# Conditioning weights dealt over three feed-forward stages instead of two, with VectorE's share of that work in smaller portions

## The reference, cut to what matters

```python
for l in range(DEPTH):
    mod_lat = (silu(c) @ w_ada[l] + b_ada[l]).reshape(b, 9, D)
    mod_ctx = (silu(c_ctx) @ w_ada[l] + b_ada[l]).reshape(1, 9, D)
    x  = _post(x,  _swiglu(_pre(x,  g[0], mod_lat, 0), ffn1_gu[l], ffn1_down[l]), g[1], mod_lat, 0, 0.5)
    xc = _post(xc, _swiglu(_pre(xc, g[0], mod_ctx, 0), ffn1_gu[l], ffn1_down[l]), g[1], mod_ctx, 0, 0.5)
    ...
    x  = _post(x,  _swiglu(_pre(x,  g[4], mod_lat, 2), ffn2_gu[l], ffn2_down[l]), g[5], mod_lat, 2, 0.5)
```

## Time and profile before

| what | value |
| --- | --- |
| median of 3 runs | 2853.93 us (2853.24 to 2855.41) |
| the profiled execution, its own time | 2855.19 us |
| its span | 2853.2 us, granted clock 0.969 |
| TensorE matmul busy | 2685.9 us, 94% of the span |
| VectorE busy | 1676.4 us, 59% |
| ScalarE, GpSimd busy | 716.0 us, 25%; 819.5 us, 29% |
| shares of the chain that ended last | TensorE 84%, VectorE 11%, of it adaW L541 3% |

### The profile page before, as it was taken

How to read it: one execution, slowest core, us unless ns; L and a number is a source line. 1 busy time by engine, 2 the same in 40 slices (tenths; PEclk the granted TensorE clock), 3 DMA queues, 4 the chain that set the end, 5 groups by cost and what they waited for, 6 DMA issues and landing times.

```text
span 2853.2 us, 39518 instructions
## 1 busy us (share of the span) xinstructions
PE 2685.9 (94%) x16446; PEld 2502.7 (88%) x16446; DVE 1676.4 (59%) x2235; ACT 716.0 (25%) x977; POOL 819.5 (29%) x1292
## 2 busy tenths in 40 slices
PE   5999999998899889999999799999999799899997
PEld 4899999998779789999999699999999668588885
DVE  5867876875582676766765643343344694644444
ACT  4211121112423431111111322112212324322222
POOL 1247776641050200000000227757641041100001
PEclk9899999999999999999999899999999899899998
DMA  9443444442445134344342232223223456133331
GB/s 315 126 132 123 152 137 142 126 165 97 138 154 163 52 104 126 107 129 126 104 126 82 74 74 80 91 91 97 82 93 111 158 160 192 59 96 96 96 96 52
DMA packets 340457, 337.07 MB, mean 118 GB/s; under 512 B 52528, under 2 KB 311224, under 8 KB 336696
## 3 DMA queue, kind: packets, MB, share of 16 engines
q1 hardware_dynamic: 279224, 204.07, 24.4%
q10 hardware_dynamic: 51840, 77.07, 8.1%
q0 software_dynamic: 9216, 53.42, 5.0%
HBM read 290.02 MB, written 44.50 MB: 117 GB/s over the span
## 4 chain that ended last, share of the span: by engine, by line
PE 84%; DVE 11%; ACT 2%; issue 2%; DMA 0%; POOL 0%; SPq 0%; ACTq 0%; DVEq 0%; POOLq 0%
PE ps L454 74%; DVE adaW L541 3%; PE ps L1394 2%; PE ps L582 2%; PE ps L1089 2%; ACT wH L439 1%; PE ps L1419 1%; DVE tmpN L1168 1%; DVE wL L446 1%; DVE rmsX L1177 1%; DVE xT L1049 1%; PE ps L1361 1%; PE ps L1074 1%; PE ps L1408 1%; DMA xin<-in_x_dram 0%
## 5 line engine op out<-in xcount | busy, mean ns | idle before, releaser
L454 PE MATMUL ps<-hH,wH 128*128 128x384 f32 (+1 forms) x2928 | 1020.1, 348 | 54.4 <-DVE hL L1186 48.1
L454 PE MATMUL ps<-hL,wH 128*128 128x384 f32 (+1 forms) x2928 | 1012.5, 346 | 0.0
L454 PE MATMUL ps<-hH,wL 128*128 128x384 f32 (+1 forms) x2928 | 1011.9, 346 | 0.0
L446 DVE TENSOR_TENSOR wL<-raw,wH 128x1024 fp32r<-128x1024 f32 x300 | 392.4, 1320 | 542.1 <-ACT wH L439 541.6
L454 PEld LDWEIGHTS ps<-hH,wH 128*128 128x128 f32 x2928 | 556.7, 190 | 81.1 <-issue 55.7
L454 PEld LDWEIGHTS ps<-hL,wH 128*128 128x128 f32 x2928 | 556.6, 190 | 17.9
L454 PEld LDWEIGHTS ps<-hH,wL 128*128 128x128 f32 x2928 | 556.1, 190 | 18.4
L454 PE MATMUL ps<-midH,wH 128*128 128x384 f32 (+1 forms) x1232 | 426.9, 346 | 12.6 <-DVE wL L446 9.9
L454 PE MATMUL ps<-midH,wL 128*128 128x384 f32 (+1 forms) x1232 | 424.2, 344 | 0.0
L454 PE MATMUL ps<-midL,wH 128*128 128x384 f32 (+1 forms) x1232 | 424.2, 344 | 0.0
L439 ACT ACTIVATE wH<-raw 128x1024 fp32r<-128x1024 f32 x300 | 310.7, 1050 | 420.8 <-PE ps L454 399.3
(11 more groups left out here) (257 smaller groups left out, 2384.9 us busy)
## 6 DMA issues: line engine op xcount, KB each, us to landing
raw<-in_ffn_gu_dram SPq DMA_DIRECT2D x176, 512.0 KB, 3.9
adaW<-in_w_ada_dram ACTq DMA_DIRECT2D x40, 1536.0 KB, 6.9
raw<-in_ffn_down_dram SPq DMA_DIRECT2D x88, 512.0 KB, 3.6
x_d<-xT POOLq DMA_DIRECT2D x4, 3072.0 KB, 9.6
xT<-x_d POOLq DMA_DIRECT2D x4, 3072.0 KB, 11.0
W_d<-gW POOLq DMA_DIRECT2D x16, 512.0 KB, 3.9
VT_d<-gVT ACTq DMA_DIRECT2D x16, 512.0 KB, 3.0
raw<-in_w_in_dram SPq DMA_DIRECT2D x16, 512.0 KB, 6.0
```

Source lines behind the costliest of these rows:

```text
L446: nc.vector.tensor_tensor(wL[:, n % SPLIT_SLOTS, :], raw[:, n % RAW_SLOTS, :], wH[:, n % SPLIT_SLOTS, :].bitcast(f32), ALU.subtract).then_ ...
L454: ins = nc.tensor.matmul(dst, a, b, start=first and n == 0, stop=last and n == 3 * len(pairs) - 1)
```

## The change

Rides 8 to 21 are put in FFN A, 22 to 33 in FFN B, 34 to 47 in FFN C. VectorE's steps come in portions behind its own work ("hooks"): up to 4 behind each `split_lo` and each `up` of a round, and one behind each addition L747. A ride's column sums stand on TensorE ahead of the first unit that finds all 16 steps early enough in VectorE's order, and this can be any of the four units; an up unit's columns are taken by ScalarE in `up`.

```diff
+    HOOK_SHARES = (4, 4, 4, 4) + (1,) * KC
+    LEAD_SHARES = (0, 0, 2, 4)
+    def share_after(s, hook):
+        if s < 0:
+            return sum(LEAD_SHARES[:hook + 1])
+        return sum(LEAD_SHARES) + s * sum(HOOK_SHARES) + sum(HOOK_SHARES[:hook + 1])
+    def share_before_unit(s, i):
+        if i == 3:
+            return share_after(s, 0)
+        return share_after(s - 1, (4 + 3, 4 + 6, 4 + KC - 1)[i] if s else i)
+    LAST_SHARE = share_before_unit(NPH - 2, 3)
+    def steps_due(n_rides, share):
+        return min(STEPS * n_rides, STEPS * n_rides * share // LAST_SHARE)
+    def place_rides(rides):
+        units = [(s, i) for s in range(NPH - 1) for i in range(4)]
+        at = {}
+        for k, R in enumerate(rides):
+            at[next(u for u in units if steps_due(len(rides), share_before_unit(*u)) >= STEPS * (k + 1) and u not in at)] = R
+        return at
...
-    F1_0 = make_ffn("f10", 0, ffn1_gu, ffn1_down, 0, 8, True)
+    F1_0 = make_ffn("f10", 0, ffn1_gu, ffn1_down, 0, range(8, 22), True)
-    F2_0 = make_ffn("f20", 0, ffn2_gu, ffn2_down, 0, 28, False)
-    F1_1 = make_ffn("f11", 1, ffn1_gu, ffn1_down, 0, None, True)
+    F2_0 = make_ffn("f20", 0, ffn2_gu, ffn2_down, 0, range(22, 34), False)
+    F1_1 = make_ffn("f11", 1, ffn1_gu, ffn1_down, 0, range(34, 48), True)
...
+        def free_tile(g):
+            if g >= F.slots:
+                wait_tile(pe, F, g - F.slots)
+            if g - F.slots in ride_in:
+                pe.wait_ge(ada_taken, ride_in[g - F.slots] + 1)
...
+        def take_ride(g, ride):
+            if ride is not None:
+                take_columns(act, ride, 2 * tile_slot(F, g), TOK // 2)
+                next_ride(ride + 2)
...
-        def up(i, f):
+        def up(i, g, f, ride):
             act.wait_ge(up_read, F.n0["up_read"] + f + 1)
+            take_ride(g, ride)
             nc.scalar.activation(midH[:, f % 4, F.tok0:TOK], midF[:, f % 2, F.tok0:TOK], ACT.Copy).then_inc(mid_hi, 1)
...
+        def ada_until(s, hook):
+            if not F.rides:
+                return
+            n = len(F.rides)
+            for step in range(steps_due(n, share_after(s, hook - 1)), steps_due(n, share_after(s, hook))):
+                ada_step_of(dve, F.rides[step // STEPS], step % STEPS)
...
             for m in range(KC):
-                if ride is not None:
-                    ada_steps(dve, ride, KC + m, KC + m + 1)
...
                                         sb_pair(yT[:, m, :], F.tok0), ALU.add).then_inc(down_read, 1)
+                if p < NPH - 1:
+                    ada_until(p, 4 + m)
...
         for s in range(NPH - 1):
-            more = F.ride0 is not None and s < NPH - 2
-            if F.ride0 is not None:
-                ada_steps(dve, F.ride0 + 2 * s + 1, 0, STEPS)
             for j in range(2):
-                if j and more:
-                    ada_steps(dve, F.ride0 + 2 * s + 2, 0, KC)
                 split_lo(dve, F.base + i + 3)
+                ada_until(s, 2 * j)
                 up(i + 1, g + 1, f)
-            down(8 + 6 * s, 8 + 12 * s, s, F.ride0 + 2 * s + 2 if more else None)
+                ada_until(s, 2 * j + 1)
+            down(8 + 6 * s, 8 + 12 * s, s)
```

More of the change, by code:

```diff
@@ L232, in build @@
     unit = 0
+    STEPS = 2 * KC
     NPH = FC // 2
@@ L338, in make_spill, with make_ffn @@
         return made["spill"]
-    def make_ffn(tag, layer, gu, down, tok0, ride0, gen):
+    def make_ffn(tag, layer, gu, down, tok0, rides, gen):
         nonlocal unit
         F = Section("ffn", FFN_COUNTS)
-        F.tag, F.layer, F.tok0, F.ride0, F.base = tag, layer, tok0, ride0, unit
+        F.tag, F.layer, F.tok0, F.base = tag, layer, tok0, unit
+        F.rides = rides
+        F.ride_of = place_rides(rides)
         unit += 6 * (FC // 2)
@@ L381, in build @@
     pre_first.sq = sq_first
-    F1_0 = make_ffn("f10", 0, ffn1_gu, ffn1_down, 0, 8, True)
+    F1_0 = make_ffn("f10", 0, ffn1_gu, ffn1_down, 0, range(8, 22), True)
     M0 = make_mixer("m0", 0, F1_0.gen)
-    F2_0 = make_ffn("f20", 0, ffn2_gu, ffn2_down, 0, 28, False)
-    F1_1 = make_ffn("f11", 1, ffn1_gu, ffn1_down, 0, None, True)
+    F2_0 = make_ffn("f20", 0, ffn2_gu, ffn2_down, 0, range(22, 34), False)
+    F1_1 = make_ffn("f11", 1, ffn1_gu, ffn1_down, 0, range(34, 48), True)
     M1 = make_mixer("m1", 1, F1_1.gen)
-    F2_1 = make_ffn("f21", 1, ffn2_gu, ffn2_down, CTX, None, False)
+    F2_1 = make_ffn("f21", 1, ffn2_gu, ffn2_down, CTX, range(0), False)
     plan = []
@@ L510, in build @@
     FIRST_RIDES = 8
-    FFN_RIDES = 20
     def ada_source(layer, ride_in_layer):
@@ L519, in ada_dma, with ada_step_of @@
         act.dma_start(adaW[:, R % 2, :, :], ada_source(*divmod(R, RIDES))).then_inc(ada_ready[R % 2], 16)
-    STEPS = 2 * KC
-    def ada_steps(dve, R, first, last):
+    def ada_step_of(dve, R, i):
         before = STEPS * (R - FIRST_RIDES)
         w = adaW[:, R % 2]
[L528 to L542, removed]
+        k, v = i // 2, 1 - i % 2
+        needed = before + (i if i < 4 else i - 1)
+        if needed:
+            dve.wait_ge(ada_step, needed)
+        if i == 0:
+            dve.wait_ge(ada_ready[R % 2], 16 * ((R - FIRST_RIDES) // 2 + 1))
+            ins = nc.vector.tensor_scalar(adaP[:], w[:, 0], siluC[:, 0, 0:1], None, ALU.mult)
+        elif i == 1:
+            ins = nc.vector.tensor_scalar(w[:, 0], w[:, 0], siluC[:, 0, 1:2], None, ALU.mult)
+        else:
+            at = w[:, 1 - v]
+            ins = nc.vector.scalar_tensor_tensor(at, w[:, k], siluC[:, k, v:v + 1], adaP[:] if i == 3 else at, ALU.mult,
+                                                 ALU.add)
+        ins.then_inc(ada_step, 1)
     def ada_ride(pe, R, bank, col):
@@ L612, in ffn_tensor, with gate_up @@
     def ffn_tensor(pe, F, pre):
-        def gate_up(i, g, ride):
+        ride_in = {4 + 12 * s + i: R for (s, i), R in F.ride_of.items()}
+        def free_tile(g):
             if g >= F.slots:
                 wait_tile(pe, F, g - F.slots)
+            if g - F.slots in ride_in:
+                pe.wait_ge(ada_taken, ride_in[g - F.slots] + 1)
+        def gate_up(i, g, ride):
+            free_tile(g)
             if ride is not None:
@@ L631, in down @@
             for m in range(KC):
-                wait_tile(pe, F, g + m - F.slots)
+                free_tile(g + m)
                 for h, (t0, w) in enumerate(halves(F.tok0)):
@@ L646, in ffn_tensor @@
             for i in range(4):
-                ride = F.ride0 + 2 * s + i // 2 if F.ride0 is not None and i % 2 == 0 else None
-                gate_up(4 + 6 * s + i, 4 + 12 * s + i, ride)
+                gate_up(4 + 6 * s + i, 4 + 12 * s + i, F.ride_of.get((s, i)))
             piece = s - 1 if F.gen and 1 <= s <= PIECES else None
@@ L671, in next_ride @@
         def next_ride(R):
-            if R < F.ride0 + FFN_RIDES:
+            if R in F.rides:
                 ada_dma(act, R)
-        if F.ride0 is not None:
[L677 to L683, removed]
+        def take_ride(g, ride):
             if ride is not None:
@@ L686, in gate @@
                 next_ride(ride + 2)
+        if F.rides:
+            act.wait_ge(h_lo, KC * F.pre.nth + KC)
+            next_ride(F.rides[0])
+            next_ride(F.rides[0] + 1)
+        def gate(i, g, f, ride):
+            act.wait_ge(w_used, F.base + i + 1)
+            take_ride(g, ride)
             if f >= 2:
@@ L700, in ffn_scalar @@
             gate(2 * j, 2 * j, j, None)
-            up(2 * j + 1, j)
+            up(2 * j + 1, 2 * j + 1, j, None)
         for s in range(NPH - 1):
             for j in range(2):
-                i, f = 4 + 6 * s + 2 * j, 2 + 2 * s + j
-                gate(i, 4 + 12 * s + 2 * j, f, None if F.ride0 is None else F.ride0 + 2 * s + j)
-                up(i + 1, f)
+                i, g, f = 4 + 6 * s + 2 * j, 4 + 12 * s + 2 * j, 2 + 2 * s + j
+                gate(i, g, f, F.ride_of.get((s, 2 * j)))
+                up(i + 1, g + 1, f, F.ride_of.get((s, 2 * j + 1)))
             piece = s - 1 if F.gen and 1 <= s <= PIECES else None
@@ L735, in up, with down @@
                                     midH[:, f % 4, F.tok0:TOK].bitcast(f32), ALU.subtract).then_inc(mid_lo, 1)
-        def down(i, g, p, ride=None):
+        def ada_until(s, hook):
[4 more added lines that the diff above has]
+                ada_step_of(dve, F.rides[step // STEPS], step % STEPS)
+        def down(i, g, p):
             for m in range(KC):
-                if ride is not None:
-                    ada_steps(dve, ride, KC + m, KC + m + 1)
                 if m < KC - 1:
@@ L753, in ffn_vector @@
         for j in range(2):
-            if F.ride0 is not None:
-                ada_steps(dve, F.ride0, j * KC, (j + 1) * KC)
             split_lo(dve, F.base + 2 * j + 3)
+            ada_until(-1, 2 * j)
             up(2 * j + 1, 2 * j + 1, j)
+            ada_until(-1, 2 * j + 1)
         for s in range(NPH - 1):
-            more = F.ride0 is not None and s < NPH - 2
```

(8 more changed lines are left out.)

## The result

| | before | after |
| --- | --- | --- |
| median | 2854.11 us (4 runs) | 2872.11 us (4 runs, 2869.49 to 2874.42) |
| ratio | | 1.0064, 95% interval 1.0052 to 1.0076 |
| profiled execution, its span | 2855.19, 2853.2 us | 2871.68, 2869.9 us |
| granted clock | 0.969 | 0.972 |
| DVE busy | 1676.4 us | 1667.8 us |

Forecast was 2866 us, range 2842 to 2886. In the chain of waits of the changed kernel (start us, length us, engine tile line, instructions) the ends of the three FFNs are found as in the earlier trace rows. L485 is the line of the matmuls now, L609 that of the column sums, L792 that of the additions, L769 and L773 those of `midF` and `midL`.

A forecast was written before the change was run, and what follows sets the result against it. TensorE, 94% busy, was taken to lose 30.6 us in FFN A to late VectorE. -29.9 - 0.6 + 33.5 + 3.4 + 5.4 = +11.8 us on 2855.2; by the median 2866 us, range 2842 to 2886.

The forecast's parts named there:

- Taken away: TensorE's waits for VectorE's ride steps and additions, with slowed matmuls behind them, go: -29.9 us in FFN A, -0.6 in B.
- cover of 0.3 us: FFN B: tile 4 due at 1092.7, addition 0 done at 1092.3 with three more steps, so no cost there.
- The fourth portion: Four steps behind a round's last `up` delay down tile 3 in FFN A and C: +33.5 us; ScalarE's column-taking +3.4.
- The margin of 0.26 us: FFN A, down tile 3: slack before the first addition delays TensorE if no step stands ahead; four steps cost 1.86 us.
- GpSimd beside the steps: VectorE steps before the first addition fall in GpSimd's quiet part, 0.53 us each; its large operations could stretch them.
- The other end: Steps before the first addition take 1.09 us each in every round, beside GpSimd's large operations: 40 us more.
- Loads: Rounds 1 and 3 of FFN A and C: VectorE waits some 4 us for ride loads; cost 0, at worst 16 us.
- The clock: TensorE's clock falls behind three of eighteen new waits at down tile 3: +5.4 us, ends 0 and 32.
- the bracket: TensorE idle gaps: 1.5 us left the clock alone, 2.45 us cost 1.8 us; the new waits lie between.
- The not-slower one: TensorE's waits for steps go and steps before the first addition cost nothing: 2823 us; with a halfway case, chance 0.20.
- The clock rival: Most new TensorE waits throw the clock, or GpSimd stretches steps beyond 2.5 us: 2876 to 2906 us, chance 0.17.
- The small one: Slack at down tile 3 is 0.5 us rather than 0.26 and no clock falls: 2856 us, chance 0.10.

The follow-up runs named there:

- portion 0: Changed kernel with VectorE portions 5, 5, 6, 0 instead of 4, 4, 4, 4, so no steps ahead of the first addition: 2823.97 us, ratio 0.9897.

## Why the prediction was right, and its one mis-sized term

**Taken away.** Predicted -29.9 us in FFN A and -0.6 in FFN B beside the rides. With portion 0, FFN A is 594.1; the forecast for an A without waits is 574.6 + 17.6 + 0.7 = 592.9. That holds to 1.2 us, by terms that cancel: 2.3 us more in the rounds, as in FFN C, 0.4 more in the first 132 matmuls, and 1.6 less in the last 96, where the clock held (16.95 against 18.52). FFN B was to be 584.1 - 10.1 - 0.6 = 573.4 and is 574.2, of which 1.2 us are the first 132 matmuls (25.91 against 24.68 before). Its cover of 0.3 us held but for round 6, with four steps and a ride at unit 3, where one tile starts 0.26 us late.

**The fourth portion.** 33.5 + 3.4 = 36.9 us of waits were predicted, 18 in number; 18 came, of 36.1 us. Moving the four steps took all of them away, and one and two steps gave waits in proportion. The margin of 0.26 us, read from one round, was good from round 3 on: the gaps are 1.72 to 1.73 us in rounds 4, 6 and 8 and 2.17 to 2.18 in rounds 3, 5 and 7, in both FFNs. FFN A and FFN C were to last near 612 us each and last 617.5 and 618.2; the term for the clock, below, has most of that.

**GpSimd beside the steps.** Taken at 0.53 us a step, as between GpSimd's large operations. In the rounds shown above it was so. The exceptions are early, as the text said: the longest wait, 2.44 us in FFN C, is in round 2, without a ride at unit 3; there the four steps take 2.41 us from the first one's start to the addition (1798.22 to 1800.63), beside GpSimd's 128x128 operations, against 2.11 in round 3 of FFN A. The other end, 1.09 us a step, was priced too low: in the five steps it was read from, the last ran after GpSimd's operations had ended (353.9), and seven that ran wholly beside such operations before the change took 10.04 us from 115.36 on, 1.43 each. As the steps fell in the quiet part, this cost the forecast nothing.

**Loads.** VectorE waits for loads of rides five times in the changed kernel (us in total, times, longest us), and TensorE has no wait behind any of them:

```profile
DVE adaP L562 <- DMA adaW<-in_w_ada_dram: 12.7, 5, 3.9
```

The forecast said some 4 us each in rounds 1 and 3 of A and C, and no cost. In round 1 they are 3.75 and 3.85 us; in round 3 there is 0.24 us in A and none in C, and two that it didn't name are in FFN B, 2.01 and 2.85. No cost is right: with portion 0, where VectorE waits 3.87 and 3.98 us for loads in round 1, TensorE has no wait in the rounds of A or C.

**The clock** is the term that was too small: a fall behind 3 of 18 waits, 5.4 us. Seven came. In the chain of waits of the changed kernel the 12 matmuls of tile 3 take 2.38 us where the clock holds; where it fell they take about 3.8:

```profile
204.20 3.63 PE ps L485 x12
...
318.51 2.38 PE ps L485 x12
...
373.43 2.38 PE ps L485 x12
...
542.91 3.87 PE ps L485 x12
...
1744.55 3.81 PE ps L485 x12
...
1801.63 3.62 PE ps L485 x12
...
1860.48 3.86 PE ps L485 x12
```

The other two are in round 0, where 60 matmuls took 12.27 and 12.23 us instead of the 10.70 that they take in FFN A of the kernel with the columns taken later. With some 1.6 us each (3.87 - 2.38 = 1.5 in the tile, the rest in the transposes behind it) this is 11 us. It agrees with the experiments: between portions 4 and 0 FFN A and FFN C differ by 23.4 + 24.1 = 47.5, of which the waits for the additions are 36.1, and 11.4 are left.

The forecast took 1.5 us of idle time as harmless and 2.45 as harmful. The length of the wait alone does not decide it. TensorE's timeline has these gaps (at the end of a row) ahead of tile 3, and the last ahead of the last 96 matmuls of FFN A:

```profile
145.34 0.44 PE L485 MATMUL ps<-midH,wH 128*128 128x384 f32 x1 [1.80 <-DVE yT L792]
...
261.25 0.44 PE L485 MATMUL ps<-midH,wH 128*128 128x384 f32 x1 [2.31 <-DVE yT L792]
...
485.62 0.45 PE L485 MATMUL ps<-midH,wH 128*128 128x384 f32 x1 [1.73 <-DVE yT L792]
...
667.35 0.45 PE L485 MATMUL ps<-midH,wH 128*128 128x384 f32 x1 [2.47 <-DVE wL L477]
```

The clock fell behind both gaps of 1.80 (round 0), behind none of the six near 1.73, behind four of the eight near 2.18, and in round 2 behind 2.44 in FFN C and not behind 2.31 in FFN A. It held behind the 2.47 us at the ends of FFN A and FFN C (96 matmuls in 16.93 and 16.94) and fell there in FFN B (18.39); before, it fell in all three (18.50, 18.50, 18.52). So the bracket did not hold, and three falls of eighteen was a guess inside it.

**What evened out.** With the measured waits and falls the forecast's sum is 36.1 - 30.5 + 11 = 16.6, and 18.0 was measured in the medians. That it comes so near is in part luck. The three FFNs moved by 20.8 in the profiled executions, by terms that the forecast did not have: 2.3 us in the rounds of A and of C, -1.6 at the end of each of the two, and 1.2 at the start of B, in sum 2.6; some 0.1 us by which each of the 18 late tiles starts later than its gap says is most of the rest. The stages outside the FFNs moved by -4.3, which no term had either.

**The rivals.** The not-slower one, 2823 us for a change whose fourth portion costs nothing, did not come, but its time was right: with that portion gone, 2824 us. The clock rival, most of the waits throwing the clock, did not come either: 7 of 18 did, and 2872 lies under its 2876; it had the direction in which the forecast was off. The small one, with a margin of 0.5 us and 2856, falls by the margin.

## What to carry to other kernels

Background work that is dealt into an engine's order must be placed by the deadline of the instruction behind it, not evenly: here one step of 0.53 us ahead of the first addition of a down part was already 0.27 us too much, while 5 steps three additions later cost nothing. VectorE is 58% busy in the changed kernel; the share says nothing about that margin. Before moving work into a stage that runs without waits, look there for the instruction whose reader is due soonest, and leave nothing ahead of it.

## What the runs showed of the hardware that was not expected

Waits of one length between two runs of dense 128x128x384 matmuls threw TensorE's clock from 2.4 to 1.2 GHz in some rounds and left it alone in others, with the same code: gaps near 2.18 us did in four of eight cases, rounds 1 and 7 of FFN A against its rounds 3 and 5. A longer wait was not the worse one in each case. In the kernel with the columns taken later the clock held behind the two longest gaps (2.65 us in round 2 of FFN A, 2.44 in round 2 of FFN C) and fell behind one of 1.75 and one of 1.74. So the cost of a wait of 1.7 to 2.5 us is not fixed: its own length, or some 1.6 us more with the slow matmuls behind it. What decides between the two these runs don't show. With one and two steps ahead of the addition the gaps were 1.38 us at most, and the clock fell behind none of the 36. That is no safe length for every place: in the kernel before, where a ride's column sums (12 matmuls of one column in the trace) stand behind the wait, 96 matmuls took 19.41 us behind a gap of 1.50 us and 18.33 behind one of 0.59. The Trainium skill (TensorE: Matmul & The Clock Gate, section Why this matters for your kernels) names a longer gap before throughput drops; these rows have it behind 1.74 to 2.47 us.
